# Delta rule of the second block: filler matmuls placed between the matmuls of a chunk's state and output, one behind each head

## What is computed

```python
def step(state, inp):
    q_i, k_i, u_i, w_i, g_i, qk_i = inp
    v_new = u_i - jnp.einsum("bhck,bhkv->bhcv", w_i, state)
    o_i = (jnp.einsum("bhck,bhkv->bhcv", q_i * jnp.exp(g_i)[..., None], state)
           + jnp.einsum("bhcs,bhsv->bhcv", qk_i, v_new))
    g_last = g_i[..., -1]
    k_dec = k_i * jnp.exp(g_last[..., None] - g_i)[..., None]
    state = state * jnp.exp(g_last)[..., None, None] + jnp.einsum("bhck,bhcv->bhkv", k_dec, v_new)
    return state, o_i
```

## Time and profile before

| | |
|---|---|
| runs | 2135.64, 2143.36, 2143.70 us |
| the profiled execution's own time | 2150.71 us |
| its span, from the first to the last instruction | 2148.9 us |
| mean granted TensorE clock over the span | 0.965 |
| TensorE busy | 2032.4 us (95% of the span) |
| VectorE, ScalarE, GpSimd busy | 900.9, 776.8, 690.8 us |
| the delta rule's steps 0 to 3 | from 1433 to 1634 us of the span |

### The profile page before, as it was taken

How to read it: one execution, slowest core, us unless ns; L and a number is a source line. 1 busy time by engine, 2 the same in 40 slices (tenths; PEclk the granted TensorE clock), 3 DMA queues, 4 the chain that set the end, 5 groups by cost and what they waited for, 6 DMA issues and landing times.

```text
span 2148.9 us, 25115 instructions
## 1 busy us (share of the span) xinstructions
PE 2032.4 (95%) x9802; PEld 1657.5 (77%) x9802; DVE 900.9 (42%) x1385; ACT 776.8 (36%) x1105; POOL 690.8 (32%) x203
## 2 busy tenths in 40 slices
PE   7987999999988999999999988989999998999999
PEld 5755978888876779788888865768888776888887
DVE  2996611121373556211213828354452425514233
ACT  5644422232354534222322546452222523222221
POOL 4870044444213200444433220221112333444443
PEclk9998999999999999999999979998899999999999
DMA  4201332322212201222223120111112221222222
GB/s 172 79 20 60 90 116 80 113 92 87 99 35 69 79 12 70 104 91 99 96 98 118 70 78 1 55 44 40 40 49 89 79 98 60 97 98 98 98 93 83
DMA packets 30239, 169.20 MB, mean 79 GB/s; under 512 B 3619, under 2 KB 5956, under 8 KB 13252
## 3 DMA queue, kind: packets, MB, share of 16 engines
q1 hardware_dynamic: 30148, 167.91, 22.2%
HBM read 162.13 MB, written 5.77 MB: 78 GB/s over the span
## 4 chain that ended last, share of the span: by engine, by line
PE 78%; DVE 11%; issue 5%; ACT 3%; POOL 1%; DMA 1%; DVEq 0%; POOLq 0%; SPq 0%; ACTq 0%
PE ps L1600 57%; PE ps L1621 5%; PE ps L1901 3%; DVE ps L1087 2%; PE ps L1557 2%; POOL wlo L418 1%; PE ps L1680 1%; ACT whi L467 1%; DMA wraw<-stream 1%; PE ps L2011 1%; PE ps L1999 1%; PE ps L1801 1%; PE ps L1789 1%; PE ps L1941 1%; PE ps L1818 1%
## 5 line engine op out<-in xcount | busy, mean ns | idle before, releaser
L418 POOL TENSOR_TENSOR wlo<-wraw,whi 128x2048 fp32r<-128x2048 f32 (+4 forms) x151 | 629.2, 4167 | 1424.1 <-ACT whi L467 1424.1
L1600 PE MATMUL ps<-xh,whi 128*128 128x512 f32 x1236 | 495.6, 401 | 25.3 <-DVE xl L925 11.8
L1600 PE MATMUL ps<-xl,whi 128*128 128x512 f32 x1236 | 485.2, 393 | 0.0
L1600 PE MATMUL ps<-xh,wlo 128*128 128x512 f32 x1236 | 485.0, 392 | 0.0
L467 ACT ACTIVATE whi<-wraw 128x2048 fp32r<-128x2048 f32 (+4 forms) x163 | 285.2, 1750 | 422.3 <-PE ps L1600 404.3
L1600 PE MATMUL ps<-hh,whi 128*128 128x512 f32 x752 | 294.6, 392 | 6.1 <-DVE hl L1115 4.2
L1600 PEld LDWEIGHTS ps<-xh,whi 128*128 128x128 f32 x1236 | 234.9, 190 | 84.5 <-POOL wlo L418 21.4
L1600 PE MATMUL ps<-hh,wlo 128*128 128x512 f32 x752 | 293.1, 390 | 0.0
L1600 PE MATMUL ps<-hl,whi 128*128 128x512 f32 x752 | 293.1, 390 | 0.0
L1600 PEld LDWEIGHTS ps<-xl,whi 128*128 128x128 f32 x1236 | 235.0, 190 | 52.6 <-issue 4.6
L1600 PEld LDWEIGHTS ps<-xh,wlo 128*128 128x128 f32 x1236 | 234.6, 190 | 49.9
(11 more groups left out here) (282 smaller groups left out, 2719.7 us busy)
## 6 DMA issues: line engine op xcount, KB each, us to landing
wraw<-stream SPq DMA_DIRECT2D x132, 1024.0 KB, 4.8
wraw<-stream SPq DMA_DIRECT2D x12, 768.0 KB, 4.2
wraw<-stream SPq DMA_DIRECT2D x6, 384.0 KB, 3.4
resid<-x SPq DMA_DIRECT2D x4, 512.0 KB, 6.7
wraw<-stream SPq DMA_DIRECT2D x8, 256.0 KB, 3.0
branch_scratch<-RS SPq DMA_DIRECT2D x8, 256.0 KB, 2.1
wraw<-stream SPq DMA_DIRECT2D x4, 512.0 KB, 3.9
out<-resid SPq DMA_DIRECT2D x4, 512.0 KB, 2.7
```

What stands on the lines that cost most here:

```text
L418: pool.tensor_tensor(wlo[:, p, 0:w], wraw[:, p, 0:w], whi[:, p, 0:w], ALU.subtract).then_inc(lo_ready, 1)
L1600: ins = pe.matmul(ps[:, 2 * p + n, :], wt[:, p, w], xt[:, k0 + k, :], start=k == 0 and q == 0, stop=k == k_tiles - 1 and q == 2)
```

## The change

Within `chunk_out` one filler follows each head's S matmul. Among the outputs one filler precedes each head's pair in the even chunk, and every second head's in the odd chunk. These fillers are taken from the blocks around: the even chunk's blocks shrink from 6 and 6 to 2 and 2, and the block of 6 ahead of the odd chunk goes. The counts per step stay (12 and 6), and so does the order among the fillers. In step 0 the same 12 and 6 are issued as before. The two last chunks behind the loop are called without fillers and stay.

```diff
-            def chunk_out(n):
+            def chunk_out(n, beside=0):
...
                 pe.wait_ge(new_ready, n + 1)
                 for h, hp in heads:
                     pe.matmul(ps[:, STATE, hp], k_rev[par][r, hp], v_new[r, hp], start=True, stop=True)
+                    if beside:
+                        side(1)
                 for h, hp in heads:
+                    if beside > 4 or (beside and h % 2 == 0):
+                        side(1)
                     cs = slice(h * P + n % 2 * DN_CH, h * P + (n % 2 + 1) * DN_CH)
...
-                side(6)
+                side(2)
                 if t:
-                    chunk_out(2 * t - 2)
-                side(6)
+                    chunk_out(2 * t - 2, 8)
+                else:
+                    side(8)
+                side(2)
                 pe.wait_ge(a_ready, t + 1)
...
-                    if lv == 0:
+                    if lv == 0 and t:
+                        chunk_out(2 * t - 1, 4)
+                    if lv == 0 and t == 0:
                         side(6)
-                    if lv == 0 and t:
-                        chunk_out(2 * t - 1)
                 side(6)
```

## The result

The changed kernel takes 2155.61 us (median of 7 runs, 2149.2 to 2168.99), the one before 2140.16 us in the same comparison (7 runs, 2135.64 to 2143.7). The ratio is 1.0079, 95% interval 1.0049 to 1.0110: 15 us slower, where +15 was forecast.

What follows compares the result with a forecast made beforehand. TensorE was taken to bound the kernel (78% of the chain that ended last). Shape changes 7.2, lost cover 2.8, state wait 1.5 and clock 3.6 made 15 us, so 2143.4 + 15 = 2158 us, range 2137 to 2169.

Steps and rivals of the forecast that it cites:

- the slower case: For the whole kernel: slower by more than about 0.5% (11 us), given a chance of 0.62.
- Part 1: Six more changes between 64 and 128 rows in each of six chunks, 0.2 us apiece, 7.2 us in all.
- Part 2: Four fillers leave the wait for VectorE's new values ahead of each even chunk's S matmuls; 2.8 us in all.
- Part 3: Transposes after the even chunk wait for VectorE's state update, covered by two fillers instead of six; 1.5 us in all.
- Part 4: Even chunks lose more at 1.2 GHz, from the last S-and-filler groups on; 3.6 us in all, odd chunks left unchanged.
- A: Fillers among short matmuls keep the clock up in all six chunks' outputs; 2130 or 2137 us, chances 0.08 and 0.07.
- B: Gaps at changes between fillers and S are hidden, the clock goes as before; 2149 us, chance 0.2.
- C: Low clock spreads to odd chunks from their S matmuls on, gaps grow to 0.35 us; +25 us, 2168 us, chance 0.1.

Runs made afterwards that it cites:

- s_only: The kernel before with one filler behind each S matmul and none among the outputs, 6 still ahead of the even chunk; 1.0070 of before.
- s_pairs: s_only with two fillers behind every second S matmul in place of one behind each; 1.0020 of the kernel before.
- grouped: The kernel before with outputs ordered by depth (all 64-row ones behind S, then all 128-row ones), start/stop flags adapted, no filler moved; 0.9908 of before.
- c2_10: The kernel before with 2 fillers ahead of the even chunk and 10 behind it; 0.9990 of before.
- after_c6: The changed kernel with 6 fillers ahead of the even chunk, 2 among its outputs and none behind it; 1.0078 of the kernel before.
- out_only: The kernel before with fillers among the outputs alone, 6 ahead of the even chunk, 2 behind it, 2 ahead of the odd one; 0.9977 of before.
- out_c2: out_only with 2 fillers ahead of the even chunk and 6 behind it; 1.0002 of the kernel before.
- after_again: The changed kernel itself, unaltered, timed in a second comparison; 1.0081 of the kernel before.

## Why the prediction was right

The forecast was 2158 us, +15 on the median known then, and the slower case. Point by point:

- **Part 1, the changes of shape**: 0.2 us each, six more per chunk, 7.2 us. Shown: 0.20 us by the pitch of S and filler, 0.17 us by s_only's steps. s_pairs and grouped, which have fewer changes than s_only and than the kernel before, move the time the way of the number (grouped with other flags besides). In the outputs a change costs 0.13 us, nearer to the 0.14 that the rows gave for them than to the 0.2 used.
- **Part 2, the lost cover**: the wait was to grow from 4.4 to 7 us, and is 7.1. In the steps that costs its 2.7 us (c2_10's are 2.6 longer); for the whole kernel the timings give between -2 and +5 us, and do not settle it.
- **Part 3, the wait for the state**: 1.5 us were taken, 0.5 measured. The clock stayed low there, and the two fillers last 1.02 us in step 1 (0.85 at 1.2 GHz was forecast, without the gap behind O2) and cover more. after_c6 shows that the wait is real when nothing covers it (3.9 us).
- **Part 4, the clock**: 3.6 us were taken, 6.1 measured. It fell where forecast, but came back later than I worked out: its low stretch took in w_state and level 0 too, for which I had no term. So the even chunks lost some 12 us more to the clock, not 3.6. The odd chunks, which I left as they were, lost 5 us less. The two partly cancel, which the forecast did not foresee.
- **The sum**: parts 1 to 3 were 11.5 in the sum and 10.0 in the windows. With the clock that is 1.5 us too much and 2.5 us too little, which nearly cancelled. The sum is better than its terms: the changes of shape were foreseen, but the agreement to 1 us is luck.
- **The rivals**: A asked that fillers among the short matmuls keep the clock up. This holds for the outputs of the odd chunks: in out_only and out_c2 the clock did not fall there in any of six, and out_only gains 5 us. With fillers between the S matmuls it is the reverse: s_only has 53 us at 1.2 GHz against 39. Each of these fillers brings two gaps; that the gaps are the reason was not tested. B (no gaps) is excluded by the pitch. C's spread of the low clock over the odd chunk did not come in the changed kernel's two traces: in step 2 the low clock reaches its first S and ends there, and in steps 1 and 3 it is over before. It did come in step 3 of after_c6, where the odd chunk ran at 1.2 GHz throughout, so C can happen. Its price was added up too low: 36 changes at 0.35 in place of 0.2 us are 5.4 us, not 4.
- **The rule**: the Trainium skill says ("TensorEngine Tiling (Array Packing)", Key Properties) that changing the tiling mode drains the engine, which spoke against the change. The traces agree, if 64 and 128 rows are two such modes: a change cost 0.20 us among the S matmuls and 0.13 us among the outputs, at 2.4 GHz. They show the gap; that it is a drain they do not show.

## What to carry to other kernels

Here a filler matmul was cheap only beside neighbours of its own depth: between matmuls with 64 rows of contraction (the depth over which a matmul sums), a filler with 128 costs 0.4 us of gaps for 0.23 us of work. So try first to order short matmuls by their depth (here that gave 0.9%), then place fillers at the seams, and ahead of a wait rather than behind it. Judge by the pitch from start to start: the busy time shows none of these gaps (3.00 of 3.00 us in the outputs).

## What had not been expected

In its trace the grouped kernel gained much more through the clock (13.7 us) than through its gaps (5.2 us); 6 us at most had been forecast for the clock. Before, TensorE counted as busy for 3.00 of 3.00 us in the odd chunk's outputs, and its clock fell at the last of them; with the gaps gone the same matmuls are through sooner, and it fell once in a step. What decides when it falls was not measured.

The changed kernel's runs spread over 20 us, and the spread is not in the part that was changed. The profiled executions of after_again (span 2149.7 us) and of the changed kernel (2167.2 us), the same program, have steps 1 to 3 of 178.2 and 178.0 us. They part ahead of step 1, in the stretch from 1225 us to its start, which takes in the delta rule's step 0. (The changed kernel's ten records more here are ten fewer before 1225 us.) Changed kernel first, then after_again:

```profile
1225.00:1474.50 249.50, 219.89 (x1009) 170.43 (x1008) 124.89 (x325) 123.67 (x247) 48.85 (x12) 0.89 0.13 47
```

```profile
1225.00:1457.00 232.00, 201.63 (x999) 155.09 (x998) 122.53 (x324) 123.16 (x246) 47.27 (x11) 0.96 0.14 50
```

17.5 us lie between them, and the clock accounts for it: 249.5 x 0.89 and 232.0 x 0.96 are 222 and 223 us, the same work at 2.4 GHz. A single execution, then, says nothing here about a change of 10 us. Its windows around the changed part say more: those two agree to 0.2 us.
